# One hybrid layer in fp32: the late half of a gather between the first expert pair's products, weight pieces and tail in another order

## The reference

```python
x = x + y @ w_out
x = x + hier_moe(rms_norm(x, norm2_g), ...)
# hier_moe, dense form; combine holds 2 weights a token
hid = silu(einsum('td,edf->tef', t, w1)) * einsum('td,edf->tef', t, w3)
hid = hid * combine[..., None]
out = einsum('tef,efd->td', hid, w2)
return rms_norm(x, final_g)
```

## Time and profile before

| | us |
|---|---|
| median of 3 runs | 1207.65 (1207.59 to 1207.99) |
| the profiled execution | 1207.29 |
| its span, first to last instruction | 1205.5 |
| PE busy | 1173.3 (97%) |
| DVE busy | 700.5 (58%) |
| ACT busy | 379.0 (31%) |
| POOL busy | 44.9 (4%) |
| DMA, mean over the span | 280 GB/s |
| idle of PE put down to weights of the experts (DMA w_b) | 12.2, in 10 waits |

### The profile page before, as it was taken

How to read it: one execution, slowest core, us unless ns; L and a number is a source line. 1 busy time by engine, 2 the same in 40 slices (tenths; PEclk the granted TensorE clock), 3 DMA queues, 4 the chain that set the end, 5 groups by cost and what they waited for, 6 DMA issues and landing times.

```text
span 1205.5 us, 18956 instructions
## 1 busy us (share of the span) xinstructions
PE 1173.3 (97%) x7316; PEld 886.3 (74%) x7316; DVE 700.5 (58%) x1024; ACT 379.0 (31%) x406; POOL 44.9 (4%) x53
## 2 busy tenths in 40 slices
PE   8999999999999999999999999999999999999995
PEld 8888888888888888888898888655555454545552
DVE  5778555556566767676886656444444444434445
ACT  5444433334444353543434543100101110000103
POOL 1000001001002022000000000000000000000002
PEclk9999999999999999999999999999999999999998
DMA  8665565765855555455664896999999999999996
GB/s 301 194 194 189 180 201 177 203 198 176 215 171 158 169 174 162 153 174 178 204 211 116 277 403 259 350 417 432 431 432 432 430 432 429 434 431 431 425 418 247
DMA packets 161707, 337.70 MB, mean 280 GB/s; under 512 B 13552, under 2 KB 139648, under 8 KB 148352
## 3 DMA queue, kind: packets, MB, share of 16 engines
q1 hardware_dynamic: 154544, 335.69, 75.8%
q10 hardware_dynamic: 7120, 1.42, 0.6%
HBM read 334.97 MB, written 2.12 MB: 280 GB/s over the span
## 4 chain that ended last, share of the span: by engine, by line
PE 82%; DMA 14%; DVE 1%; issue 1%; SPq 0%; ACT 0%; POOL 0%; POOLq 0%; DVEq 0%; ACTq 0%
PE ps L1056 20%; PE ps L1405 14%; DMA w_b<-in_w_dram 14%; PE ps L1086 12%; PE ps L1059 10%; PE ps L1089 6%; PE ps L1214 4%; PE ps L1437 4%; PE ps L1216 2%; PE ps L1446 2%; PE ps L1339 1%; PE ps L1447 1%; PE ps L1031 1%; PE ps L1178 0%; DMA xin<-in_x_dram 0%
## 5 line engine op out<-in xcount | busy, mean ns | idle before, releaser
L1533 DVE TENSOR_TENSOR wsplit<-wraw,wsplit 128x2048 fp32r<-128x2048 f32 x119 | 273.6, 2299 | 176.2 <-ACT wsplit L724 176.1
L724 ACT ACTIVATE wsplit<-wraw 128x2048 fp32r<-128x2048 f32 x119 | 228.1, 1917 | 368.3 <-PE ps L1059 194.1
L1056 PE MATMUL ps<-act_split,wsplit 128*128 128x512 f32 x1024 | 323.2, 397 | 0.0
L1405 PE MATMUL ps<-w_a,xe_a 128*64 128x256 f32 x960 | 219.8, 385 | 12.5 <-DMA w_b<-in_w_dram 12.2
L1059 PEld LDWEIGHTS ps<-act_split,wsplit 128*128 128x128 f32 x1024 | 192.4, 188 | 45.4
L1405 PE MATMUL ps<-w_b,xe_b 128*64 128x256 f32 x960 | 219.9, 385 | 0.0
L1405 PEld LDWEIGHTS ps<-w_a,xe_a 128*64 128x64 f32 x960 | 129.8, 138 | 98.1 <-DMA w_b<-in_w_dram 21.0
L1059 PE MATMUL ps<-act_split,wsplit 128*128 128x256 f32 x1024 | 201.3, 278 | 0.0
L1086 PE MATMUL ps<-wsplit,act_split 128*128 128x512 f32 x608 | 191.9, 397 | 0.0
L1056 PEld LDWEIGHTS ps<-act_split,wsplit 128*128 128x128 f32 x1024 | 156.4, 189 | 0.9 <-issue 0.4
L1089 PEld LDWEIGHTS ps<-wsplit,act_split 128*128 128x128 f32 x608 | 114.2, 188 | 26.9
(11 more groups left out here) (315 smaller groups left out, 1127.3 us busy)
## 6 DMA issues: line engine op xcount, KB each, us to landing
wraw<-in_w_in_dram SPq DMA_DIRECT2D x88, 1024.0 KB, 5.1
w_a<-in_w_dram SPq DMA_DIRECT2D x37, 2048.0 KB, 15.4
w_b<-in_w_dram SPq DMA_DIRECT2D x37, 2048.0 KB, 19.5
wraw<-in_w_out_dram SPq DMA_DIRECT2D x16, 1024.0 KB, 6.5
w_a<-in_w_dram SPq DMA_DIRECT2D x14, 1024.0 KB, 12.7
w_b<-in_w_dram SPq DMA_DIRECT2D x14, 1024.0 KB, 15.1
wraw<-in_w_branch_m_dram SPq DMA_DIRECT2D x8, 1024.0 KB, 5.1
wraw<-in_w_branch_a_dram SPq DMA_DIRECT2D x8, 1024.0 KB, 5.2
```

The costliest lines, as they stand in the source:

```text
L724: act.activation(wsplit[:, q % 2, :, 0], wraw[:, q % RAW], ACT.Copy).then_inc(rounded, 1)
L1056: pe.matmul(banks[b], w[:, k, 0, b * P:(b + 1) * P], act_of(q, k), start=first and k == 0, stop=False)
L1405: last = pe.matmul(ps[b * SLOTS:(b + 1) * SLOTS, 2 * w, 0:FF], operands[b][:, k], w13[b][:, w, k], start=k == 0, stop=k == DC - 1)
L1533: dve.tensor_tensor(wsplit[:, q % 2, :, 1], wraw[:, q % RAW], wsplit[:, q % 2, :, 0].bitcast(F32), ALU.subtract).then_inc(split, 1)
```

## The change

Five edits, all in the last 560 us of the program:

1. **w_out.** `turn_x2(0, 0)`, which stood ahead of `out_pair(1)`, comes after the first half of it, and `route(0, 0)` after the second half.
2. **Pair 0.** One late bank after each part (0, 1, 2, 3), then `turn`, the w2 products of column groups 0 and 1, banks 4 to 7, and the products of groups 2 and 3. DVE now makes `hid` (`up(0)`) ahead of bank 5 but behind bank 3 and the first piece of `make_x2`, and copies `xe_a` of pair 1 early, `xe_b` at the end. ACT copies bank 4 and rounds the first two column groups ahead of bank 6.
3. **Loads.** Pair 1's w1 and w3 all come in quarters (1 MiB for the two experts), each as soon as that quarter of pair 0 is used; w2 of pair 2 in two pieces of 1024 columns; w1 and w3 of pair 2 by parts of 2 MiB. Pairs 1 and 2 are written out ahead of PE's loop because their wait values differ.
4. **Tail, PE.** The last pair's column groups 2 and 3 are done apart with two scatters between them, and the last two scatters do both `ys_hi` products first and then both `ys_lo` products.
5. **Tail, layout.** `x3` is gone: `tail_add` writes `x2` in place, in channel order. POOL makes 4 groups of `x2g` and DVE the fifth; they and the last three scalings on DVE read `fin_g` and write `x2g` or `fin` with the step of 16 elements.

```diff
@@ SP
-                for part in range(1, PARTS):
-                    parts_done(1, part)
-                    for b in range(2):
-                        load_part(b, 2 + b, part)
-                for n in range(4):
-                    sp.wait_ge(y_summed, 4 * (chunks - 1) + n + 2)
-                    cols = slice(n * 512, (n + 1) * 512)
+                for part in range(PARTS):
+                    w, h = divmod(part, 2)
+                    for quarter in range(2):
+                        if quarter == 0:
+                            sp.wait_ge(mid_parts, (chunks - 1) * PARTS + (part + 1))
+                        else:
+                            parts_done(1, part)
+                        first = (2 * h + quarter) * (DC // 4)
+                        for b in range(2):
+                            load_steps(b, 2 + b, w, first, first + DC // 4, w13_loaded[w][h])
+                for n in range(2):
+                    sp.wait_ge(y_summed, 4 * (chunks - 1) + 2 * n + 3)
+                    cols = slice(n * 1024, (n + 1) * 1024)
...
                 for i in range(2, HALF_LEAD - 1):
-                    next_hidden(i)
+                    if i == 2:
+                        for part in range(PARTS):
+                            parts_done(2, part)
+                            for b in range(2):
+                                load_part(b, 4 + b, part)
+                    else:
+                        next_hidden(i)
@@ POOL
-            for g, (t, n) in enumerate(tail_groups[:LAST_COLUMNS]):
+            for g, (t, n) in enumerate(tail_groups[:GAINED]):
...
-                pool.tensor_tensor(x2g[:, t, cols], x3[:, t, cols], fin_g[:, cols], ALU.mult).then_inc(x2g_ready, 1)
+                pool.tensor_tensor(in_order(x2g[:, t, cols]), columns(x2, t, n), in_order(fin_g[:, cols]),
+                                   ALU.mult).then_inc(x2g_ready, 1)
@@ ACT
-                    gathered(1, (2, 4, 6))
+                    gathered(1, (2,))
                     turn_hidden(0)
+                    gathered(1, (4,))
+                    act.wait_ge(x2_whole, 1)
+                    ys_round(0, 0, 2)
+                    gathered(1, (6,))
@@ PE, out_pair and what stood ahead of it
-                    route(i - 1, u)
+                    first = isinstance(i, int) and i == 1 and u == 0
+                    if first:
+                        turn_x2(0, 0)
+                    else:
+                        route(i - 1, u)
...
+                    if first:
+                        route(0, 0)
                     turn_x2(1 - u, i * 2 + (u - 1))
...
-            turn_x2(0, 0)
@@ PE, pair 0
-                hidden(0, 0, (xg[:, :, 0:SLOTS], xe_first), [[lambda js=js: gather_late(js)] for js in ((0, 1), (2, 3), (4, 5), (6,))])
+                hidden(0, 0, (xg[:, :, 0:SLOTS], xe_first), [[lambda j=j: gather_late((j,))] for j in range(PARTS)])
                 turn(0)
-                gather_late((7,))
+                pe.wait_ge(xg_act, N_BANKS // 2 + 2)
+                rows(0, 0, 0, (0, 1))
+                gather_late((4, 5, 6, 7))
                 pe.wait_ge(xg_act, N_BANKS)
-                rows(0, 0, 0)
+                rows(0, 0, 0, (2, 3))
@@ PE, tail
-                rows(None, LAST, 1, (2, 3), w2_last)
+                rows(None, LAST, 1, (2,), w2_last)
                 tail_scatter((2, 3), 2)
+                rows(None, LAST, 1, (3,), w2_last)
                 tail_scatter((4, 5), 3)
-                tail_scatter((6, 7), 4)
+                pe.wait_ge(ys_rounded, LAST * 2 + 4)
+                for g in (6, 7):
+                    pe.wait_ge(x2_final, g - 3)
+                    scatter_high(tail_banks[g % 4], 1, *tail_groups[g])
+                pe.wait_ge(ys_ready, LAST * 2 + 1 + 4)
+                for g in (6, 7):
+                    scatter_low(tail_banks[g % 4], 1, *tail_groups[g]).then_inc(scattered, 1)
@@ DVE, pair 0
                 gathered(1, (3,))
                 gate(0)
                 make_x2(*late_chunks[0])
+                up(0)
+                starts_at = starts_of(1, 0)
+                dve.wait_ge(x2_whole, 1)
+                copy_tokens(starts_at, 1, (0,))
                 gathered(1, (5,))
                 make_x2(*late_chunks[1])
-                up(0)
-                starts_at = starts_of(1, 0)
                 gathered(1, (7,))
                 make_x2(*late_chunks[2])
                 all_gathered()
-                copy_tokens(starts_at, 1)
+                copy_tokens(starts_at, 1, (1,))
@@ DVE, tail
-                    dve.tensor_tensor(columns_of_x3(t, n), columns(x2, t, n), columns_now(tail_banks[g % 4]),
-                                      ALU.add).then_inc(x2_final, 1)
+                    cols = columns(x2, t, n)
+                    dve.tensor_tensor(cols, cols, columns_now(tail_banks[g % 4]), ALU.add).then_inc(x2_final, 1)
...
+                tail_add((2,))
                 ys_split_part(LAST * 2 + 3, 2, 3)
-                tail_add((2,))
+                tail_add((3,))
                 ys_split_part(LAST * 2 + 4, 3, 4)
-                tail_add((3, 4, 5, 6, 7))
+                tail_add((4, 5, 6, 7))
...
+            dve.tensor_tensor(in_order(x2g[:, t, cols]), columns(x2, t, n), in_order(fin_g[:, cols]), ALU.mult).then_inc(x2g_ready, 1)
             dve.wait_ge(squares3, GROUPS_OUT)
```

More of the change, by code:

```diff
@@ L396, in layer @@
         LAST_COLUMNS = 5
+        GAINED = LAST_COLUMNS - 1
         DVE_SQUARES = (0,)
@@ L1397, in hidden @@
                         pe.wait_ge(xe_ready, part + 1)
-                    second_halves = {0: 32, LAST - 1: 96, LAST: 128}.get(i, 64) if isinstance(i, int) else 64
-                    quarters = 32 if w == 0 and not (isinstance(i, int) and i == 0) else 0
+                    second_halves = {0: 32, 1: 96, LAST - 1: 160, LAST: 192}.get(i, 128) if isinstance(i, int) else 128
+                    quarters = 0 if isinstance(i, int) and i == 0 else 32
                     pe.wait_ge(w13_loaded[w][h], second_halves if h else i * 32 + (32 + quarters))
@@ L1429, in rows @@
                 if pieces is None:
-                    pieces_more = 96 if slot == 0 and not (isinstance(load_no, int) and load_no == 0) else 0
+                    pieces_more = 32 if slot == 0 and not (isinstance(load_no, int) and load_no == 0) else 0
                     pe.wait_ge(w2_loaded[slot], load_no * 32 + (32 + pieces_more))
@@ L1490, in hidden_and_scatter @@
                     scatter(i - 1, half, (6, 7))
-                with pe.Fori(0, N_PAIRS // 2 - 2) as j:
+                hidden_and_scatter(1, 0)
+                rows(0, 1, 1)
+                hidden_and_scatter(2, 1)
+                rows(1, 2, 0)
+                with pe.Fori(1, N_PAIRS // 2 - 2) as j:
                     hidden_and_scatter(j * 2 + 1, 0)
```

58 lines of the change are left out of this document (30 added, 28 removed).

## The result

The changed kernel took 1213.49 us (median of 6 runs, 1212.67 to 1215.49); the kernel before, in the runs beside it, 1207.62 (1207.35 to 1210.84, 6 runs). The ratio is 1.0045, interval 1.0034 to 1.0055: slower by 5.4 us, 4.1 to 6.6 (5.9 between the medians). Forecast were 1210.1 and a range up to 1212.2: the direction was right, but +2.4 is less than half of what came, and the time lies above the range. The profiled execution took 1213.29 with a span of 1211.5.

A forecast was written before the change was run, and what follows sets the result against it. PE was taken to lead up to about 784 us, the expert-weight stream after. Pair 0 5.0, w_out -0.35 and lead -1.8 make 2.85; tail -0.45 gives +2.4 on 1207.65: 1210.1 us, own range 1209.3 to 1211.2, wider 1207.2 to 1212.2.

The forecast's parts named there:

- pair 0 5.0: Pair 0 on PE: the new order makes pair 1 start 5.0 us later, at 779.45 instead of 774.46.
- w_out -0.35: w_out's products ahead of pair 0: the reorder gains 0.35 us on PE, bounds 0 and 0.75.
- the lead -1.8: Weight stream at w2 of pair 3: it takes in 1.8 us of PE's lateness, bounds 1.3 to 2.5.
- the tail -0.45: End of the kernel: sum of squares 1.55 us earlier, scalings 1.1 longer, so -0.45; POOL adds nothing.
- The wait in pair 0: PE idles 4.1 us at `turn(0)` near 763 us, until DVE's `hid` is ready at 767.3.
- Then `turn` ... rows start at 768.25. Half of 7.09 is 3.55: Pair 0 behind the wait: `turn` 0.2 us, first half of the w2 products 3.55, ending at 771.8.
- The two sizes that were worked out from rows: Tail: sum of squares starts 1.55 us earlier; the three stepped scalings on DVE cost 1.1 more.
- A: Rival: PE does not stand at `turn(0)`, the quartered loads carry through and the stream decides: 1204.8 us; chance 10%.
- B: Rival, tail: stepped POOL groups take 2.1 us each and the root waits 0.5 or more: 1210.6 to 1212.2; 20%.
- C: Rival: PE waits, but lead is 2.5 us, w_out gives 0.75, tail -0.8: about 1208.6 us; chance 20%.

The follow-up runs named there:

- run 5: Changed kernel with 16 fp32 matrix calls that nobody reads put ahead of `turn(0)`: 1211.62 us, ratio 1.0027 to the kernel before.
- run 10: Changed kernel without the loading edits, all else as changed: 1213.58 us, ratio 1.0039 to the kernel before.
- run 6: Kernel before with the loading edits alone: 1208.57 us, ratio 1.0001.
- run 8: Kernel before with the loading and tail edits, without those of pair 0 and w_out: 1206.89 us, ratio 0.9987.
- run 9: Changed kernel timed again with no edit: 1213.30 us, ratio 1.0036 to the kernel before.
- run 1: Kernel before with the w_out edit alone: 1208.32 us, ratio 1.0001.
- run 2: Kernel before with the two tail edits alone: 1206.63 us, ratio 0.9988.
- run 11: Changed kernel with DVE's first piece of x2 behind `up(0)`, bank 3's copy and the gate still ahead: 1210.40 us, ratio 1.0010 to the kernel before.

## Why the prediction was right and wrong

Term by term, against the forecast's sum of +2.4 (pair 0 5.0, w_out -0.35, the lead -1.8, the tail -0.45):

- **The wait in pair 0: right.** Place, releaser and length (4.1, measured 4.07) are as forecast, and so are the pieces behind it (banks 4 to 7: 4.0, measured 4.03; second half 3.55, measured 3.63). Run 5 gives pair 1's start as forecast.
- **The step that failed: "Then `turn` ... rows start at 768.25. Half of 7.09 is 3.55".** That prices work behind a wait at the clock it had without the wait. The half took 5.41, because the clock was at 0.50 for most of it, and `turn` 0.69 in place of 0.44. Together +2.0, shown by run 5 by itself. This is the largest error and alone brings 2.4 to 4.4.
- **The lead of 1.8: too large by 0.65 in the stream** (the table under run 10), and not seen in the time at all (runs 6, 8 and 10: 0.1, 0 and 0.3). The forecast took the spare time in SP's queue, worked out from two issues and a rate, for the stream's lead. That the stream sets the end holds in the profile of the changed kernel, but not in every execution: in run 9 PE is the end, after a slow clock behind its last long wait.
- **w_out: 0.19 instead of 0.35 up to the second unit, and nothing that can be told in the time** (run 1). Left out was the wait of ACT for the weights of w_out, right behind the point at which the forecast's path ended. Nothing is the forecast's own lower bound.
- **The tail: -1.5 instead of -0.45** (run 2). The two sizes that were worked out from rows held (sum of squares 1.55, measured 1.64 to 1.66; a stepped scaling 1.1, measured 1.04). What failed is the sum: the scalings were put on the path at full length, and the stores cover them, so they cost 0.1 to 0.2.
- **The rivals.** A did not come: PE stood. B's price is off: a stepped group on POOL costs 1.53, not 2.1, and the root never waits for it. C had the right idea of the tail (-0.8) and the wrong one of the lead.

The right terms make 5.0 + 2.0 - 1.15 - 1.5 = 4.4, which lies inside the changed kernel's interval near its lower end; with no lead (runs 6 and 10) it is 5.5, at its middle. Which of the two holds for the time stays open.

**The rows were there.** The kernel before shows the mechanism that was left out. PE's timeline and the windows, in a wait for weights of the steady stage:

```profile
1078.56 0.43 PE L1405 MATMUL ps<-w_a,xe_a 128*64 128x256 f32 x1 [2.54 <-DMA w_b<-in_w_dram]
```

```profile
1076.00:1078.00 2.00, 0.02 (x2) 0.00 (x0) 0.88 (x1) 1.02 (x1) 0.00 (x0) 1.00 1.00 426
1078.00:1079.00 1.00, 0.44 (x4) 0.34 (x6) 0.35 (x1) 0.00 (x0) 0.00 (x0) 1.00 1.03 442
1079.00:1083.00 4.00, 4.00 (x24) 2.36 (x22) 0.00 (x0) 0.00 (x0) 0.00 (x0) 0.57 0.98 418
```

PE waits 2.54 us, starts again at 1.00, and then runs four microseconds at a mean of 0.57. There it costs the time nothing, because the stream sets the pace and DMA goes on at 418. In the earlier trace rows it is only a mean of 0.99. In pair 0 PE sets the pace, and the same fall is paid in full.

It does not come behind every such wait. The same trace has one of like length with the clock at 1.00 behind it:

```profile
937.50 0.43 PE L1405 MATMUL ps<-w_a,xe_a 128*64 128x256 f32 x1 [2.53 <-DMA w_b<-in_w_dram]
```

```profile
937.00:941.00 4.00, 3.50 (x32) 2.21 (x32) 0.30 (x1) 0.00 (x0) 0.00 (x0) 1.00 1.01 434
```

In all fourteen traces together the clock fell behind 30 of 44 waits for expert weights of 2.5 to 2.6 us, behind one of 8 of 1.7 to 2.0 us, and behind none of 6 of 1.3 to 1.6 us. So the rows of before could tell that the wait of 4.1 us was likely to cost some 2 us more, not that it had to. Whoever forecasts a new wait of PE should look for its like in the trace and read the clock behind it; with the 2.0 of run 5 that would have put the forecast at 1212.1. The other corrections (lead 0.65, w_out 0.35, tail -1.05) nearly cancel out; with no lead at all it is 1213.2, against 1213.49 measured.

The Trainium skill, "TensorE: Matmul & The Clock Gate", section "HAM oscillation — how this bites in real kernels", says that in a kernel whose tiles are short against the wait for their data, the engine is put to its slow clock in the wait and begins the next tile slow. This case agrees in kind, with 0.50 in and behind the wait of 4.07 us and 2.0 us lost; behind the waits of 2.54 and 1.87 us shown here the fall came only when the engine was at work again.

The Trainium skill, "GPSIMD Engine Reference", section "Performance pitfalls for Q7 kernels", gives about half as much again for reads with a large step. Here one stepped read (`fin_g`) and a stepped write (`x2g`) made it 1.53 in place of 1.26 to 1.39, a tenth to a fifth more; the measurement decides.

## What to carry to other kernels

Before an instruction that releases TensorE is put behind others, count what stands ahead of it on its own engine once the thing that covered them has moved: here two instructions of DVE made a reorder cost 7 us that costs nothing with `hid` first and the new loading. Price a new wait of TensorE with the slow clock behind it wherever TensorE sets the pace (2.0 us here behind 4.1, in four of four profiles), and shorten such a wait to nothing or fill it to size: cut to 1.87 us it still lost the clock's share in the execution profiled. At the end of a kernel ask what the stores cover before the last arithmetic is put on the path.

## What was not expected of the hardware

- The granted clock fell behind a wait of only 1.87 us (run 11), and only when PE was at work again (1.00 up to 767, 0.52 behind it; PE had started at 765.76). In the changed kernel it fell while PE stood.
- The fall did not come behind every wait of its size: behind 30 of 44 of 2.5 to 2.6 us. The last long wait, of 2.6 us, was followed by it in five of six profiles; run 5 kept 1.00 behind its own.
- A 128x128 product on fp32 by a call of its own is two records of some 0.115 us (64 in 7.31, 32 in 3.74), at full clock.
- Single executions differ by up to 1.3 us ahead of pair 0 with no edit there (743.99 to 745.30), and ACT's wait for w_out's weights ahead of it by up to 1.7 (3.6 to 5.3).
